# Two fused transformer blocks on one core: first weights split in pieces, last product turned round, zeros multiplied ahead

## The reference

```python
memn = _rmsnorm(mem, norm_mem_g)                      # 256 memory tokens
k, vm = jnp.split(memn @ w_kv, 2, axis=-1)            # keys and values, 1024 columns each
h = _rmsnorm(x, norm_mix_g)
proj = h @ w_in                                       # 9216 columns
...                                                   # mixer and FFN of the first block: x
x = _rmsnorm(x, norm_final_g)                         # end of the first block
xn = rms_norm(x, norm_g)                              # second block: windowed attention
...                                                   # o: attention output, z: gate
x = x + (merge_heads(o, B, T) * jax.nn.silu(z)) @ w_out
return rms_norm(x, final_g)
```

## Time and profile before

| | us |
|---|---|
| median of 3 runs (lowest, highest) | 1247.23 (1246.58, 1248.08) |
| the profiled execution, its own time | 1247.16 |
| its span, first to last instruction | 1245.4 |
| mean granted TensorE clock | 0.994 |
| TensorE busy | 1216.8 (98%) |
| VectorE, ScalarE, GpSimd busy | 834.8, 490.8, 19.5 |
| HBM read, written | 124.20 MB, 5.27 MB |

### The profile page before, as it was taken

How to read it: one execution, slowest core, us unless ns; L and a number is a source line. 1 busy time by engine, 2 the same in 40 slices (tenths; PEclk the granted TensorE clock), 3 DMA queues, 4 the chain that set the end, 5 groups by cost and what they waited for, 6 DMA issues and landing times.

```text
span 1245.4 us, 16229 instructions
## 1 busy us (share of the span) xinstructions
PE 1216.8 (98%) x5820; PEld 1010.5 (81%) x5820; DVE 834.8 (67%) x1271; ACT 490.8 (39%) x769; POOL 19.5 (2%) x22
## 2 busy tenths in 40 slices
PE   6899999999999999999999999999999999999996
PEld 6888888888888888888888888888888888877775
DVE  6648988877789987553457866666644444477774
ACT  6453333233243323552234533434433333165641
POOL 3100000000000000000000000000000000000000
PEclk9999999999999999999999999999999999999998
DMA  7433222222123232243322232322243534311111
GB/s 276 150 128 102 101 84 84 87 83 85 68 85 102 88 115 85 85 169 102 101 86 84 102 101 101 101 90 95 87 135 102 203 102 152 102 52 51 36 50 67
DMA packets 34258, 127.02 MB, mean 102 GB/s; under 512 B 3824, under 2 KB 4112, under 8 KB 33696
## 3 DMA queue, kind: packets, MB, share of 16 engines
q1 hardware_dynamic: 32832, 118.50, 28.1%
q0 software_dynamic: 944, 7.44, 1.7%
q10 hardware_dynamic: 432, 0.40, 0.1%
HBM read 124.20 MB, written 5.27 MB: 104 GB/s over the span
## 4 chain that ended last, share of the span: by engine, by line
PE 95%; DVE 2%; ACT 1%; POOL 1%; DMA 1%; issue 0%; SPq 0%; DVEq 0%; ACTq 0%; POOLq 0%
PE acc L745 81%; PE acc L762 6%; PE acc L779 2%; PE acc L988 1%; PE side L959 1%; PE acc L972 1%; PE side L838 1%; PE side L858 1%; POOL part L388 1%; DVE w_low L1032 1%; DMA mem_in<-mem 1%; PE side L800 0%; PE side L791 0%; DVE result L1545 0%; PE side L848 0%
## 5 line engine op out<-in xcount | busy, mean ns | idle before, releaser
L745 PE MATMUL acc<-h_high,w_high 128*128 128x512 f32 x880 | 342.8, 390 | 0.0
L745 PE MATMUL acc<-h_low,w_high 128*128 128x512 f32 x880 | 342.4, 389 | 0.0
L745 PE MATMUL acc<-h_high,w_low 128*128 128x512 f32 x880 | 342.4, 389 | 0.0
L1032 DVE TENSOR_TENSOR w_low<-w_raw,w_high 128x1024 fp32r<-128x1024 f32 x216 | 264.7, 1234 | 40.0 <-ACT w_high L422 36.5
L422 ACT ACTIVATE w_high<-w_raw 128x1024 fp32r<-128x1024 f32 x216 | 224.5, 1051 | 92.9 <-PE acc L745 89.0
L745 PEld LDWEIGHTS acc<-h_high,w_low 128*128 128x128 f32 x880 | 165.2, 188 | 34.4
L745 PEld LDWEIGHTS acc<-h_high,w_high 128*128 128x128 f32 x880 | 165.2, 188 | 34.1
L745 PEld LDWEIGHTS acc<-h_low,w_high 128*128 128x128 f32 x880 | 165.3, 188 | 33.8
L1100 DVE SCALAR_TENSOR_TENSOR convs<-long_u,par,convs 128x510 f32<-128x510 f32 (+28 forms) x232 | 170.3, 734 | 6.6
L745 PE MATMUL acc<-f_high,w_high 128*128 128x512 f32 x176 | 68.6, 390 | 0.0
L745 PE MATMUL acc<-f_low,w_high 128*128 128x512 f32 x176 | 68.5, 389 | 0.0
(11 more groups left out here) (285 smaller groups left out, 1809.9 us busy)
## 6 DMA issues: line engine op xcount, KB each, us to landing
w_raw<-weights SPq DMA_DIRECT2D x216, 512.0 KB, 3.2
rows_dram<-strip_dram POOLq DMA_DIRECT2D x1, 3072.0 KB, 14.4
x_in<-x SPq DMA_DIRECT2D x2, 1024.0 KB, 12.2
x<-x POOLq DMA_DIRECT2D x1, 2048.0 KB, 8.8
bias<-rows_dram POOLq DMA_DIRECT2D x1, 2048.0 KB, 10.4
out<-result SPq DMA_DIRECT2D x8, 256.0 KB, 2.1
mem_in<-mem SPq DMA_DIRECT2D x2, 512.0 KB, 7.3
par<-params ACTq DMA_DIRECT2D x1, 258.0 KB, 4.4
```

The costliest lines, as they stand in the source:

```text
L745: mm = pe.matmul(acc[:, bank, 0:width], w[:, s, (skip + b) * P:(skip + b + 1) * P], moving[v][:, k, :], start=first and b == 0 and w is w_ ...
L1032: dve.tensor_tensor(w_low[:, s, :], raw[s][:, :], w_high[:, s, :].bitcast(F32), ALU.subtract)\
```

## The change

The first two units and the memory come and are split in four pieces (`CHUNK`, a quarter of a unit: two channel tiles), and TensorE takes each piece when it is split. The memory comes by ScalarE's queue, ones and identity by GpSimd's. Ahead of the first piece TensorE multiplies zeros in float32, 512, 512, 512 and 256 columns. Key units 4 to 7 go to the second halves of the banks of units 0 to 3; the first two pairs of value units go to `side` and the others to `acc`. Squares of memory and x get room of their own (`mem_sq`, `x_sq`), the order of splits on ScalarE and VectorE is written out, `total` and `spread` move, and units 16 and 17 are split last. In the q, k, v projections `turn_x` transposes the residual into token layout, eight times four transposes, one `spread` goes, and VectorE writes `y_rows`. The last product has tokens on the partitions: the output tiles are stationary and the weights move; channel tiles 0 to 4 are done for all tokens, tiles 5 to 7 token tile by token tile (`last_done`). Each token tile's mean square is then a sum along the free axis. VectorE and ScalarE scale half of it each, and SP and ScalarE store half each. VectorE's chunk splits (not shown) mirror ScalarE's.

```diff
+LAST_BY_TILE = 5
+
+
+CHUNKS = 4
+CHUNK = UNIT // CHUNKS
...
+            for c in range(CHUNKS):
+                at = c * CHUNK
+                for s in range(2):
+                    sp.dma_start(raw[s][:, at:at + CHUNK], weights[s, :, at:at + CHUNK]).then_inc(first_landed[c], 16)
             for s in range(2, SLOTS):
                 sp.dma_start(raw[s][:, :], weights[s]).then_inc(landed[s], 16)
-            for i in range(2):
-                sp.dma_start(x_in[:, 4 * i:4 * i + 4, :], x[:, 4 * i:4 * i + 4, :]).then_inc(x_landed[i], 16)
-            with sp.Fori(1, ROUNDS) as m:
+
+            def load(m, s):
+                sp.wait_ge(weight_low, 4 * m + (s - 3))
+                sp.dma_start(raw[s][:, :], weights[4 * m + s]).then_inc(landed[s], 16)
+
+            def load_x(i):
+                sp.dma_start(x_in[:, 2 * i:2 * i + 2, :], x[:, 2 * i:2 * i + 2, :]).then_inc(x_landed[i], 16)
+
+            load_x(0)
+            load_x(1)
+            load(1, 0)
+            load(1, 1)
+            load_x(2)
+            load(1, 2)
+            load(1, 3)
+            load_x(3)
...
+            pool.memset(conv_sum, 0.0).then_inc(zeros_set, 1)
+            pool.dma_start(ones, consts[:, 0:P]).then_inc(consts_landed, 16)
+            pool.dma_start(ident, consts[:, P:2 * P]).then_inc(consts_landed, 16)
...
+            for k in range(1, KT):
+                pool.wait_ge(x_squared, k + 1)
+                at_least(pool, x_added, k - 1)
+                pool.tensor_tensor(x_sum, x_sum if k > 1 else x_sq[:, 0, :], x_sq[:, k, :], ALU.add)\
+                    .then_inc(x_added, 1)
...
+            load_memory(0)
             act.dma_start(par[:, :], params).then_inc(par_landed, 16)
-            act.dma_start(ones, consts[:, 0:P]).then_inc(consts_landed, 16)
-            act.dma_start(ident, consts[:, P:2 * P]).then_inc(consts_landed, 16)
-            round_high(0, 0)
-            round_high(0, 1)
...
+            for c in range(1, CHUNKS):
+                load_memory(c)
+            for c in range(CHUNKS):
+                act.wait_ge(first_landed[c], 32)
+                for s in range(2):
+                    at = c * CHUNK
+                    act.activation(w_high[:, s, at:at + CHUNK], raw[s][:, at:at + CHUNK], ACT.Copy)\
+                       .then_inc(chunk_high if c < CHUNKS - 1 else weight_high, 1)
+                if c == 0:
+                    act.wait_ge(par_landed, 16)
+                act.wait_ge(mem_landed[c], 16)
+                for k in range(2 * c, 2 * c + 2):
+                    act.activation(mem_high[:, k, :], mem_in[:, k, :], ACT.Copy, scale=col("g_mem", k))\
+                       .then_inc(act_high, 1)
...
+            unit_high(2)
+            mem_squares(0)
+            mem_squares(1)
+            unit_high(3)
+            mem_squares(2)
+            mem_squares(3)
+            x_squares(0)
+            unit_high(4, 5)
+            x_squares(1)
+            unit_high(6)
+            x_squares(2)
+            unit_high(7)
+            x_squares(3)
+            unit_high(8)
+            root(N_MEM, MEM // P)
+            unit_high(9, 10, 11)
+            root(N_X)
+            for k in range(2):
+                x_high(k)
+            take_values(0)
+            unit_high(12, 13)
+            for k in range(2, 5):
+                x_high(k)
+            take_values(1)
+            unit_high(14, 15)
+            for k in range(5, KT):
+                x_high(k)
+            take_values(2)
+            unit_high(16, 17)
+            take_values(3)
...
+            for t in range(4):
+                for half in range(2):
+                    act.wait_ge(x3_done, 2 * t + half + 1)
+                    if t or half:
+                        act.wait_ge(x3_squared, 2 * t + half)
+                    act.activation(square[:, half, :], x3[:, t, half * SEQ:(half + 1) * SEQ], ACT.Square,
+                                   accum_out=last_sum[:, t, half:half + 1]).then_inc(x3_squared, 1)
+                act.wait_ge(last_step, 2 * t + 2)
+                act.activation(last_root[:, t:t + 1], last_sum[:, t, 3:4], ACT.Sqrt, scale=float(D))\
+                   .then_inc(last_rooted, 1)
+                act.wait_ge(last_rooted, t + 1)
+                act.wait_ge(x3_gained, 2 * t + 2)
+                act.activation(result[:, t, SEQ:D], result[:, t, SEQ:D], ACT.Copy, scale=last_root[:, t:t + 1])\
+                   .then_inc(result_other, 1)
+                act.wait_ge(result_other, t + 1)
+                act.dma_start(out[t * P:(t + 1) * P, SEQ:D], result[:, t, SEQ:D]).then_inc(stored, 16)
...
+            def key_part(i, k):
+
+                s, at = i % 4, MEM * (i // 4)
+                for w, v in ((w_high, 0), (w_high, 1), (w_low, 0)):
+                    mm = pe.matmul(acc[:, s, at:at + MEM], w[:, s, k * P:(k + 1) * P], memory[v][:, k, :],
+                                   start=k == 0 and w is w_high and v == 0, stop=k == KT - 1 and w is w_low)
...
+            pe.wait_ge(zeros_set, 1)
+            for width in (SEQ, SEQ, SEQ, MEM):
+                pe.matmul(side[:, 3, 0:width], conv_sum[:, 0:P], conv_sum[:, 0:width], start=True, stop=True)
+            for k in range(KT):
+                c = k // 2
+                if k % 2 == 0 and c < CHUNKS - 1:
+                    pe.wait_ge(chunk_low, 2 * c + 2)
+                if k == 2 * CHUNKS - 2:
+                    pe.wait_ge(weight_low, 2)
+                pe.wait_ge(act_low, k + 1)
+                for i in range(2):
+                    key_part(i, k)
+            for i in range(2, 6):
+                key_unit(i)
             pe.wait_ge(consts_landed, 32)
-            for i in range(2, 2 * SLOTS):
-                product(i // 4, i % 4, memory, MEM)
-                if i == 2:
-                    total(N_MEM, MEM)
-                if i == 3:
-                    spread(N_MEM, MEM)
-                if i == X_ROOT - 1:
-                    total(N_X, SEQ)
-                if i == X_ROOT:
-                    spread(N_X, SEQ)
-            for m in range(R_KV + 2, R_LONG):
-                for s in (0, 2):
-                    rows(m, s, memory, 2)
+            total(N_MEM, MEM)
+            key_unit(6)
+            spread(N_MEM, MEM)
+            key_unit(7)
+            total(N_X, SEQ)
+            value_rows(0, 0)
+            spread(N_X, SEQ)
+            value_rows(0, 1)
+            for v in range(1, 4):
+                for t in range(2):
+                    value_rows(v, t)
...
-            spread(N_FINAL, SEQ)
+
+            def turn_x(n):
+
+                t, half = n // 2, n % 2
+                at_least(pe, y_ready, n - 1)
+                for c in range(4):
+                    mm = pe.transpose(side[:, n % 2, c * P:(c + 1) * P], x2[:, 4 * half + c, t * P:(t + 1) * P], ident)
+                mm.then_inc(y_turned, 1)
+
             product(R_QKV, 3, xn)
             for s in range(SLOTS):
+                turn_x(s)
                 product(R_QKV + 1, s, xn)
             for s in range(2):
+                turn_x(4 + s)
                 product(R_QKV + 2, s, xn)
-            rows(R_QKV + 2, 2, xn, 4, range(2))
+            turn_x(6)
+            rows(R_QKV + 2, 2, xn, 4, range(1))
+            turn_x(7)
+            rows(R_QKV + 2, 2, xn, 4, range(1, 2))
...
-            two(R_LAST, 0, (o2_high, o2_low), (gated_low, 0))
-
-            pe.wait_ge(sw_out, KT)
-            for s in range(2, SLOTS):
-                product(R_LAST, s, (o2_high, o2_low))
-            for s in range(SLOTS):
-                product(R_LAST + 1, s, (o2_high, o2_low))
-            total(N_LAST, SEQ)
-            spread(N_LAST, SEQ)
+
+            def last(k, t, half):
+
+                s, bank = k % 4, (acc if t < 2 else side)[:, 2 * (t % 2) + half, :]
+                for o, w in ((o2_high, w_high), (o2_high, w_low), (o2_low, w_high)):
+                    mm = pe.matmul(bank, o[:, k, t * P:(t + 1) * P], w[:, s, half * SEQ:(half + 1) * SEQ],
+                                   start=k == 0 and o is o2_high and w is w_high, stop=k == KT - 1 and o is o2_low)
+                return mm
+
+            pe.wait_ge(sw_step, 6 * 2 * KT)
+            for k in range(LAST_BY_TILE):
+                pe.wait_ge(weight_low, 4 * R_LAST + k + 1)
+                pe.wait_ge(gated_low, k + 1)
+                for t in (2, 3, 0, 1):
+                    if k == 0 and t == 0:
+                        pe.wait_ge(sw_own_turned, 2 * KT)
+                        pe.wait_ge(sw_older_turned, older(2 * KT))
+                    if k == 0 and t == 1:
+                        pe.wait_ge(sw_out, KT)
+                        pe.wait_ge(taken[Z_BANK], uses(R_Z, 0) + KT)
+                    for half in range(2):
+                        mm = last(k, t, half)
+                mm.then_inc(unit_done, 1)
+            pe.wait_ge(weight_low, 4 * R_LAST + KT)
+            pe.wait_ge(gated_low, KT)
+            for t in range(4):
+                for half in range(2):
```

(100 more changed lines are left out.)

222 lines of the change are left out of this document (111 added, 111 removed).

## The result

The changed kernel takes 1234.39 us (median of 4 runs, 1234.12 to 1235.38), the kernel before beside it 1247.32 (1246.58 to 1248.08). The ratio is 0.9898 (95% interval 0.9881 to 0.9915): 12.9 us faster. The forecast was 1229.5 with a range of 1227.0 to 1233.5: the direction is right, the gain 4.9 us smaller than said, and the time 0.9 above the range.

What follows compares the result with a forecast made beforehand. TensorE was taken as busy from 69.1 to 1038.7 us, leaving the opening, the q, k, v stage and the tail to change: 1247.16 - 12.6 + 2.9 - 7.95 = 1229.5 us, range 1227.0 to 1233.5.

Steps and rivals of the forecast that it cites:

- last piece "at 8.2 to 9.5", ScalarE without a gap from 4.5: Opening: pieces land in time, ScalarE copies them from 4.5 to 10.3 us, TensorE reaches unit 2 at 12.6.
- pieces land late: Rival for the opening: small piece loads come 1.2 to 5 us later, giving 1230.7 to 1234.5 us; chance 0.12.
- The roots are made while TensorE does unit 6 and the first value rows: Opening, before the value products: the roots are covered by TensorE's work, so they add no wait.
- The rest of the opening: From unit 2 at 12.6 us to round 4 at 56.5: key units, `total`, `spread`, value halves, small waits.
- the allowance of 0.6: Opening: 0.6 us added for small late waits before round 4 starts at 56.5.
- The zeros: Start of the opening: zero products end between 5.9 and 7.4 us, clock high between 5 and 8, real work from 6.9.
- The rival's 2.6 us for their absence: Rival on the zeros: clock rises some 6 us after the first real piece, costing 2.6 us, 1231.8; chance 0.12.
- q, k, v stage: Projections: 32 added transposes cost 3.8 us, one `spread` of 0.89 goes; 2.9 us lost, between 2.6 and 4.5.
- transposes cost the clock: Rival for the projections: transposes count as rest, the stage runs at 1.2 GHz, 31 us lost, 1260.6; chance 0.02.
- Last product: Final matmuls: 192 before and after, 0.2267 us apart; stationary tokens should change nothing.
- Tail: From last matmul to the end: 6.1 us in place of 14.05, 7.95 gained, bounds 5.4 and 8.
- VectorE is late by about 0.4: Tail: the table load makes VectorE late by about 0.9 us, four token tiles give back half, 0.4 remains.

Runs made afterwards that it cites:

- e2: The changed kernel with SP issuing units 2 and 3 and x only when the last piece of units 0 and 1 has landed: 1236.17 us.
- e8: The changed kernel with the memory's four loads on SP's queue, each behind its weights, ScalarE issuing only the parameters: 1234.05 us.
- e11: e8 and e5 together, with GpSimd's loads of ones and identity issued only when the last piece has landed: 1232.67 us.
- e3: The changed kernel with units 0 and 1 loaded whole, 512 KB each, still split in pieces: 1236.38 us.
- e5: The changed kernel with all seven sums of x squares on VectorE and none on GpSimd: 1233.06 us.

## Why the forecast was off

**Opening, last piece "at 8.2 to 9.5", ScalarE without a gap from 4.5: wrong, 3.2 us.** The working added up bytes, gave them the rate of a busy slice "on full engines" from 2.5 us on, and took the first piece for there before ScalarE was free. Shown: the first piece is there at 5.6 to 5.9, piece 1 at 8.45, and ScalarE waits 2.2 us behind its late start. Three things stand behind this. First the start (the last two numbers are the DMA engines' share and GB/s):

```profile
2.00:3.00 1.00, 1.00 (x2) 0.34 (x1) 0.00 (x0) 0.00 (x0) 0.63 (x2) 1.00 0.54 139
3.00:4.00 1.00, 1.00 (x2) 0.34 (x1) 0.00 (x0) 0.00 (x0) 0.00 (x0) 1.00 0.66 215
```

Then come 323, 346, 396, 381 and 358 GB/s, against 419 from 3 to 4 us before: 2.2 MB by 9 us, and 2.4 MB at 9.6. The trace of before had poor slices as well, 160 from 2 to 3 and 247 from 7 to 8, which I passed over.

Second, in e2 the waiting engine was released some 0.9 us after the last bytes had moved. Third the order: by 8.45 us 2.0 MB had come and piece 1 was only then there, though it and what is ahead of it are 1.3 MB; with all in order on one queue it is there at least 1.9 us earlier (e8). The loads behind are not to blame for the first pieces (e2), and nothing shows that the constants are (e11); the size of the loads was not isolated (e3). Order helps the first pieces only, and then unit 2's own load is the bound. How the 3.2 us divide among the three stays open.

The rival "pieces land late" named this place, at 1230.7 to 1234.5; I gave it 0.12. That this range holds the result is in part luck, for 1.9 us of the error come from the other step. The Trainium skill (DMA: Bandwidth & Descriptors, Measured) has a 64 KB load at 138 GB/s, from which the forecast estimated one microsecond of loss. The trace doesn't bear the reason out: while the pieces came the engines moved 323 to 396 GB/s from 4 us on, and what was lost lies ahead of that and in the order.

**"The roots are made while TensorE does unit 6 and the first value rows": wrong, 1.9 us.** The step took one price for VectorE's difference. The trace of before held the other: while GpSimd summed, from 22.99 on the earlier trace rows, its differences took 2.19, 1.98 and 1.95 us.

```profile
26.66 2.19 DVE L1032 TENSOR_TENSOR w_low<-w_raw,w_high 128x1024 fp32r<-128x1024 f32 x1
...
29.11 1.98 DVE L1032 TENSOR_TENSOR w_low<-w_raw,w_high 128x1024 fp32r<-128x1024 f32 x1
```

e5 gives the whole 1.9 back.

**The rest of the opening: right.** With VectorE free of GpSimd, 43.89 against 43.3 + 0.6; the allowance of 0.6 is the wait of 0.7 for units 16 and 17, there in every version with the new opening.

**The zeros: the mechanism right, the worth nothing.** They end at 6.6 (5.9 to 7.4 forecast), the first real matmul is at 7.55 (6.9), the clock is up at once. The rival's 2.6 us for their absence was wrong for a reason that the text didn't have: TensorE was waiting anyway.

**q, k, v stage: right**, 2.91 against 2.9: eight starts of four transposes at 0.44 and the granted clock 1.00, so the rival "transposes cost the clock" is refuted. **Last product: right**, 43.8 against 43.77. **Tail: right**, 6.0 against 6.1 (the end of the last matmul is modelled). That VectorE is late by about 0.4 shows in the chain, where its addition starts at 1227.15 instead of 1226.8.

**What stays open.** Why the small loads pass through a slice of 184 to 219 GB/s when all come by one queue was not separated into number of loads, row size and queue. Nor is it shown why single issues took 1.33 us in the change. An opening with unit 2 at 12.6 was not reached: the best had it at 14.8.

## What to carry to other kernels

Price an instruction from rows taken while the same neighbours run, and look for its slowest rows as well as its mean: here VectorE's difference beside GpSimd was in the trace of before, at 2.0 instead of 1.2. For an opening, list the bytes up to each consumer, not only to the first, take the rate from the first slices of a trace, where it is still rising, and add the time from the last byte to the waiting engine. A step that lies beside a wait (here the zeros) is worth nothing until that wait is gone; ask first which of the two ends last.

## What the runs showed of the hardware

Moving seven additions from GpSimd to VectorE makes VectorE finish earlier: 7 x 0.69 = 4.8 us more work, but differences of 1.23 instead of 2.03, the addition of 0.42 instead of 1.40, and no sums of 2.03 each on GpSimd to wait for.

The warm-up of e3 didn't last through its wait. The same zeros end at 6.5, TensorE then waits 3.27 us, the granted clock is 1.00 until 8 us, 0.79 in the next and 0.50 in the one after (1.2 GHz), and the matmuls start 0.21 apart from 10.11 to 15.23, 5.1 us. With waits of 0.93 and 1.08 in the change they were 0.12 apart at once. TensorE's rows and the window from 9 to 10 us in e3:

```profile
1.32 5.16 PE L935 MATMUL side<-convs 128*128 128x512 f32 x8 [1.32 <-POOL convs L414]
9.76 0.55 PE L907 MATMUL acc<-mem_high,w_high 128*128 128x256 f32 x1 [3.27 <-DVE mem_low L1292]
10.11 0.42 PE L907 MATMUL acc<-mem_low,w_high 128*128 128x256 f32 x1
...
9.00:10.00 1.00, 0.24 (x1) 0.28 (x2) 0.97 (x4) 1.00 (x4) 0.00 (x0) 0.50 1.00 385
```
